# A transformer layer on one Trainium2 core: the conditioning's partial rows summed by transposes and a reduction, in a new SBUF layout

## The chip, the cores and the metric

The kernel runs on one core of one Trainium2 chip. Its engines work side by side, each on its own queue of instructions: TensorE (PE, matrix products into PSUM), VectorE (DVE), ScalarE (ACT), GpSimd (POOL, unused here) and SyncE (SP), which issues nearly all DMAs. The metric is the device time of one execution in microseconds, as the median of several runs. The profile is of one further execution, so its durations add up to its own time and not to the median.

## The reference, cut to what matters

One layer of an encoder in float32, 256 rows of width 2048: gated feed-forward (width 5632), a mixer with two groups of eight attention heads, and a second feed-forward. Each of the three is preceded by a normalisation with a shift and a scale and followed by a gate, and these nine vectors come from the conditioning vector `c`:

```python
cond = jax.nn.silu(c)                      # (1, 2048)
mod = cond @ w_ada[l] + b_ada[l]           # (1, 9 * 2048)
sh1, sc1, gt1, sh2, sc2, gt2, sh3, sc3, gt3 = jnp.split(mod, N_MOD, axis=-1)
h = modulate(rmsnorm(x, g_ffn1_pre[l]), sh1, sc1)
y = rmsnorm(swiglu(h, w1_gate[l], w1_up[l], w1_down[l]), g_ffn1_post[l])
x = x + MACARON_WEIGHT * gt1[:, None, :] * y
# the mixer with sh2, sc2, gt2 and the second feed-forward with sh3, sc3, gt3 follow
```

## The kernel before, in words

**Products.** The 256 rows are two tiles of 128. Weights arrive in units of 256 x 512 elements (512 KB, two rows of 2 KB in each partition) in `raw`, a ring of 8 slots. Each float32 product is made of three products of rounded operands: ACT copies a unit to a rounded high piece `w_hi` (a ring of 4, line 457), DVE subtracts it and leaves the low piece `w_lo` in the place of `raw` (line 771), and PE runs high x high, high x low and low x high (lines 1254 to 1256), 12 matmuls of 512 columns for a unit. The transposed activations stand in `h_hi`/`h_lo` or, within a feed-forward, in `hid_hi`/`hid_lo`. PE's results collect in the PSUM pairs `pair0` and `pair1`. PE waits for a unit on `raw_used`, which `lo_unit` raises on DVE.

**Stages.** A first stage ("pre", four parts) makes the first shift and scale; then gate/up 1 (11 blocks, the middle ones in a hardware loop), down 1 (4 blocks), input projection ("win", 8 blocks), the two small projections and attention, output projection ("wo", 4 blocks), gate/up 2 and down 2. At the end of down 1, of wo and of down 2 `branch_end` finishes the normalisation and the residual.

**The conditioning.** The product of `cond` with `w_ada` (151 MB of weights) is made on DVE, between the rest. Its 18432 columns are 36 quarters of 512, each with 8 units (kind "A" in the plan). For a unit `ada_unit` multiplies each of its two rows by a scalar of `c_col` and adds it to a 128 x 512 accumulator (lines 787 and 790). After 8 units the 128 partitions hold 128 partial rows, which must be added up over the partitions. For the 28 quarters behind the first stage the accumulator is `acc` (two slots), for the 8 of the first stage it is `start_acc` with two partial rows in each partition.

`sum_columns` on PE (line 1314) adds them up: it waits until DVE has taken the last unit, and for the previous sums to be used (`mod_ready`), and multiplies each 128 x 128 piece by a column of ones (line 1326). The result is one column of `mps` for a piece, so the vector comes out along the partitions, where it is needed. `mod_columns` on DVE (line 809) then adds the bias from `col` and writes to `mod` (line 820), and raises `mod_ready`. In the plan PE's part stands at the end of a block and DVE's part in the next one, before the low piece of unit 3 or 4.

**Order of the queues.** It is written out by hand. `run` on DVE walks through a block's units in the order of the DMAs, and calls tasks ahead of the unit they are listed for. `transposes` (line 1288) is the helper for all other transpositions on PE: the piece of data is loaded as weights and the identity `ident` streams through, into the two halves of `tps`.

**SBUF.** Tiles are placed one behind the other in the order of their declaration. 1152 bytes of each partition are taken before the first one, so `raw` starts at byte 1152. From the sizes, `w_hi` starts at 33920, `x` at 50304, `y` at 66688, `acc` at 87168, `h_hi` at 101664 and `hid_hi` at 134432. `start_acc` and the mixer's tiles share the place of `hid_hi` and `hid_lo`.

Of the kernel before, what the change touches and what calls it, by code (L numbers as in the profile page):

```python
# [23 lines left out]
BF16 = mybir.dt.bfloat16  # L24
ALU = mybir.AluOpType
ACT = mybir.ActivationFunctionType
AX_X = mybir.AxisListType.X

P = 128
SEQ = 256  # L30
TT = SEQ // P
D = 2048
KD = D // P
FF = 5632
Q_RANK, KV_RANK = 512, 256
NOPE, ROPE, DV = 128, 64, 128
HEADS = 8
CHUNK = 64
EPS = 1e-6
N_MOD = 9  # L40
# [3 lines left out]
DB = D // NB  # L44
# [6 lines left out]
C_ID, C_TRI, C_ONE = 0, P, 2 * P  # L51
C_COS, C_SIN = 3 * P, 3 * P + TT * ROPE // 2
C_ALL = 3 * P + TT * ROPE
# [4 lines left out]
V_ROWS = 246  # L58
# [120 lines left out]
def build(nc, A, const, out):  # L179
    pl, tp, taken, order = make_plan()  # L180
    ctx = ExitStack()
    with ctx:
        def sb(name, shape, dt=F32):
            return ctx.enter_context(nc.sbuf_tensor(name, shape, dt))
# [3 lines left out]

        with nc.sbuf_tensor("raw", [P, RING, 2, NB], F32) as raw:
            pass
        w_lo = sb("w_lo", [P, RING, 2, NB], F32R)
# [4 lines left out]
        s = sb("s", [P, TT, NB])  # L198
        acc = sb("acc", [P, 2, NB])
        tmp = sb("tmp", [P, 2, NB])  # L200
        cst = sb("cst", [P, C_ALL])
        msk = sb("msk", [P, 3, P], BF16)
        col = sb("col", [P, V_ROWS])
        mod = sb("mod", [P, N_MOD * KD])
        a_col = sb("a_col", [P, KD])
        g_col = sb("g_col", [P, KD])
        c_col = sb("c_col", [P, 2, KD])
        ssq = sb("ssq", [P, TT, DB])
        ms = sb("ms", [P, TT])
        inv_ms = sb("inv_ms", [P, TT])  # L210
        newton = sb("newton", [P, TT])
        warm = sb("warm", [P, 1])
        rstd = sb("rstd", [P, TT])
        kpe = sb("kpe", [P, 2, TT, ROPE])
        fz = sb("fz", [P, 5, TT, HEADS])
        nmax = sb("nmax", [P, 2, TT])
        nbias = sb("nbias", [P, 2, TT])
        rsum = sb("rsum", [P, 2, TT])
        rinv = sb("rinv", [P, 2, TT])
        ident = cst[:, C_ID:C_ID + P]  # L220
        tri = cst[:, C_TRI:C_TRI + P]
        ones = cst[:, C_ONE:C_ONE + P]

        h_hi = sb("h_hi", [P, KD, SEQ], F32R)
        h_lo = sb("h_lo", [P, KD, SEQ], F32R)
# [19 lines left out]
            pass  # L245
        hid_hi = sb("hid_hi", [P, FF // P, SEQ], F32R)
        hid_lo = sb("hid_lo", [P, FF // P, SEQ], F32R)
        gate_mix = kv[:, 0, :]


# [9 lines left out]
        mps = ctx.enter_context(nc.psum_tensor("mps", [P, 2, NB], F32))  # L260
# [55 lines left out]
        def plus(n, i, per):  # L316

            return n + i * per if per else n
# [447 lines left out]
        def _(dve):  # L766
# [42 lines left out]
            def mod_columns(b, i=0, per_q=0):  # L809

                k, c0 = DB * len(b.sums), plus(DB * b.sums[0], i, DB * per_q)
                dve.wait_ge(sum_ready, plus(b.m + 1, i, int(per_q > 0)))
                if b in pl["pre"]:

                    c0 = DB * pl["pre"].index(b)
                    of = lambda v: v[:, 0:2 * KD].rearrange("p (v k) -> p v k", v=2)[:, :, c0:c0 + DB]
                    nc.vector.tensor_tensor(of(mod), mps[:, 0, 0:k].rearrange("p (v k) -> p v k", v=2), of(col),
                                            ALU.add).then_inc(mod_ready, 1)
                    return
                nc.vector.tensor_tensor(mod[:, bass.ds(c0, k)], mps[:, 0, 0:k], col[:, bass.ds(c0, k)],  # L820
                                        ALU.add).then_inc(mod_ready, 1)

            def power(k, width, columns, t=slice(0, TT)):
# [159 lines left out]
            def quarter_columns(e):  # L983

                mod_columns(pre[e - 1])
                dve.drain()
                k = slice(DB * (e - 1), DB * e)
                nc.vector.scalar_tensor_tensor(a_col[:, k], mod[:, KD:2 * KD][:, k], 1.0,
                                               col[:, G_PRE["ffn1"]:G_PRE["ffn1"] + KD][:, k],
                                               ALU.add, ALU.mult).then_inc(gain_ready, 1)  # L990
                dve.drain()
                return mod[:, 0:KD]
# [20 lines left out]
            for f, gu, down in (("1", "gu1", "down1"), ("2", "gu2", "down2")):  # L1013
# [12 lines left out]
                for start, count in RUNS[gu]:  # L1026
                    before, b, at = pl[gu][start - 1], pl[gu][start], 2 * (start - 1)
                    with dve.Fori(0, count) as i:
                        def last_block():
                            hidden(before, i, 16, 1)  # L1030
                            if before.sums and (b.sums or count == 1):
                                mod_columns(before, i, 1)

                        def last_hidden():
                            lo_hid(tp["hid" + f] + at, th + at, (i + (start - 1)) * 4, i, 2)
                        run(b, {4: last_block, 7: last_hidden}, i, len(b.seq), 16)
# [9 lines left out]
                if f == "1":  # L1046
                    mod_columns(last)
# [134 lines left out]
                for t in range(TT):  # L1182
                    q = y[:, t, 0:HEADS * QK].rearrange("p (h e) -> p h e", h=HEADS)
                    q1, q2 = q[:, :, NOPE:NOPE + half], q[:, :, NOPE + half:QK]
                    c, d = (v[:, t:t + 1, :].to_broadcast([P, HEADS, half]) for v in (cos, sin))
# [7 lines left out]
                for n in range(N_ATT + 6):  # L1193
# [13 lines left out]
                    if 0 <= m < N_ATT:  # L1207
# [3 lines left out]
                        for t in range(TT):  # L1211
                            k0, k1 = (0, P) if t == 0 else (P, 3 * P)
                            ins = nc.vector.tensor_scalar(prob[:, m % 4, k0:k1], prob[:, m % 4, k0:k1],
                                                          rinv[:, m % 2, t:t + 1], None, ALU.mult)
# [30 lines left out]
        def _(pe):  # L1245
# [68 lines left out]
            def sum_columns(b, i=0, per=0, per_m=0, start=None):  # L1314

                pe.wait_ge(raw_used, plus(b.r_sums(), i, per))
                if per_m or b.m:
                    pe.wait_ge(mod_ready, plus(b.m, i, per_m))
                for k in range(DB * len(b.sums)):
                    c = slice((k % 4) * P, (k % 4 + 1) * P)  # L1320
                    if start is None:
                        parts = [acc[:, b.slots[k // 4], c]]
                    else:
                        parts = [start[:, k // 4, row, c] for row in range(2)]
                    for n, part in enumerate(parts):
                        ins = nc.tensor.matmul(mps[:, 0, k:k + 1], part, ones[:, 0:1], start=n == 0,  # L1326
                                               stop=n == len(parts) - 1)
                ins.then_inc(sum_ready, 1)

            def gate_rows(t0, dg0, places):  # L1330
# [23 lines left out]
            nc.tensor.transpose(mps[:, 1, P:V_ROWS], y[0:rest, 0, P:2 * P], cst[0:rest, 0:rest]).then_inc(cols_full, 1)  # L1354
            pre = pl["pre"]
            sum_columns(pre[0], start=start_acc[:, 0])

            for e, b in enumerate(pre[1:] + pl["gu1"][:1]):
                for cp in (2 * e, 2 * e + 1):
                    turn_x(tp["mod1"], XN["ffn1"], cp)  # L1360
                for u in range(4):
                    cp = 2 * e + u % 2
                    pe.wait_ge(h_ready, HR["ffn1"] + cp + 1)
                    unit(b, u, h_hi, h_lo, 2 * cp, u // 2, cp == 0, cp == 7)
                if b.sums:
                    sum_columns(b, start=start_acc[:, (e + 1) % 2])

            for f, gu, down in (("1", "gu1", "down1"), ("2", "gu2", "down2")):
                first, t0 = pl[gu][0], tp["hid" + f]
                if f == "2":  # L1370
                    gate_up(first, ready=HR["ffn2"], ahead=lambda u: turn_ahead(tp["mod2"], XN["ffn2"], u))
                    sum_columns(first)
                pe.wait_ge(t_taken["a"], taken[t0 - 1][1])
                for start, count in RUNS[gu]:
                    before, b, at = pl[gu][start - 1], pl[gu][start], 2 * (start - 1)
# [31 lines left out]
                for n, b in enumerate(win):  # L1407
                    bank_free(b.g)
                    for u in range(8):
                        if n == 0:  # L1410
# [3 lines left out]
                             n=KV_RANK + ROPE + HEADS if n == 1 else NB)  # L1414
                        if n and u == (7 if n <= 3 else 5):
# [16 lines left out]
                            if n == 5:  # L1432
# [6 lines left out]
                                                 stop=True).then_inc(cum_full, 1)  # L1439
# [166 lines left out]
```

## Time and profile before

| | before |
|---|---|
| median of 3 runs | 2041.19 us (2041.05 to 2043.98) |
| profiled execution | 2044.09 us |
| its span | 2042.3 us |
| PE, DVE, ACT busy | 95%, 67%, 41% |
| mean granted PE clock | 0.981 |
| DMA | 488.20 MB, 239 GB/s over the span |

The span is the time between the first and the last instruction of the profile; 1.8 us of the profiled execution lie around it. Matmuls are pipelined, so that the durations of several overlap: one 128x512 matmul is recorded with some 0.39 us while the next one starts 0.23 us after it. What PE's queue pays is read from start to start, or from the chain of waits, where each piece ends with the start of the next. A group in the chain with "x8" has eight records. A time in brackets in the timeline is the engine's idle time before the instruction, and behind the arrow stands what ended it.

### The profile page before, as it was taken

The page shows a single profiled execution, that of the slowest core. Times are in us where ns is not written, and L with a number is a line of the kernel's source. Part 1 is how long each engine was busy: PE and PEld are TensorE (multiplying, and loading weights), DVE is VectorE, ACT ScalarE, POOL GpSimd, SP SyncE. Part 2 cuts the span into 40 slices and gives each one's busy share as a digit, 9 for nine tenths or more (in the row PEclk, how much of TensorE's full clock was granted, in tenths as well). Part 3 has the DMA queues.
Part 4 walks back from the last instruction along what each step waited for, and adds up shares of the span by engine and source line. Part 5 has one row for each costly group of instructions (what it writes and reads, how often), then busy time and mean ns, then how long its engine had stood idle before and what let it go on. Part 6 is the DMA issues. An engine that isn't in the chain of part 4 may idle for free.

```text
span 2042.3 us, 24582 instructions
## 1 busy us (share of the span) xinstructions
PE 1935.3 (95%) x8662; PEld 1560.7 (76%) x8662; DVE 1359.0 (67%) x1707; ACT 846.7 (41%) x1040; POOL 0.2 (0%) x4
## 2 busy tenths in 40 slices
PE   1779999999999999989999997999999999999998
PEld 1568888888887888767887776788888888788886
DVE  6877777777777667778885886777644444544444
ACT  3134433444343334354434545534344444344433
POOL 0000000000000000000000000000000000000000
PEclk9879999999999999989999998999999999999999
DMA  9878878888888778849885385787766666656663
GB/s 363 315 272 264 264 260 272 273 276 270 278 270 277 264 259 307 299 125 310 287 301 183 107 277 185 248 267 258 266 183 183 183 183 184 184 174 186 186 188 131
DMA packets 254921, 488.20 MB, mean 239 GB/s; under 512 B 17414, under 2 KB 19836, under 8 KB 254588
## 3 DMA queue, kind: packets, MB, share of 16 engines
q1 hardware_dynamic: 253968, 486.66, 72.9%
q8 instruction: 46, 0.75, 0.1%
q10 hardware_dynamic: 876, 0.53, 0.1%
q14 instruction: 31, 0.25, 0.0%
HBM read 485.04 MB, written 2.10 MB: 239 GB/s over the span
## 4 chain that ended last, share of the span: by engine, by line
PE 87%; DVE 6%; DMA 3%; DVEq 2%; ACT 1%; issue 1%; ACTq 0%; SPq 0%
PE pair L1256 28%; PE pair L1254 28%; PE pair L1255 27%; PE tps L1294 2%; DMA raw<-in_w_ada 2%; DVE start_acc L790 1%; DVEq L779 1%; PE mps L1326 1%; DVE w_lo L771 1%; DVE acc L790 1%; DMA raw<-in_w_in 1%; ACT w_hi L457 1%; PE tps L1334 0%; DMA raw<-in_w_up 0%; DVEq L1202 0%
## 5 line engine op out<-in xcount | busy, mean ns | idle before, releaser
L771 DVE TENSOR_TENSOR w_lo<-raw,w_hi 128x1024 fp32r<-128x1024 f32 x634 | 770.5, 1219 | 528.6 <-ACT w_hi L457 525.0
L457 ACT ACTIVATE w_hi<-raw 128x1024 fp32r<-128x1024 f32 x634 | 668.1, 1056 | 1021.2 <-PE pair L1256 551.8
L1254 PE MATMUL pair<-w_hi,h_hi 128*128 128x512 f32 (+1 forms) x1792 | 715.6, 399 | 38.7 <-DVE w_lo L771 36.6
L1256 PE MATMUL pair<-w_hi,h_lo 128*128 128x512 f32 (+1 forms) x1792 | 714.5, 399 | 0.0
L1255 PE MATMUL pair<-w_lo,h_hi 128*128 128x512 f32 (+1 forms) x1792 | 708.4, 395 | 0.0
L1254 PEld LDWEIGHTS pair<-w_hi,h_hi 128*128 128x128 f32 x1792 | 340.3, 190 | 121.8 <-issue 39.7
L1255 PEld LDWEIGHTS pair<-w_lo,h_hi 128*128 128x128 f32 x1792 | 340.3, 190 | 82.0 <-issue 0.2
L1256 PEld LDWEIGHTS pair<-w_hi,h_lo 128*128 128x128 f32 x1792 | 339.7, 190 | 79.7
L790 DVE SCALAR_TENSOR_TENSOR acc<-raw,c_col,acc 128x512 f32<-128x512 f32 x420 | 315.7, 752 | 53.1 <-DMA raw<-in_w_ada 20.6
L1256 PE MATMUL pair<-w_hi,hid_lo 128*128 128x512 f32 x704 | 279.6, 397 | 0.0
L1254 PE MATMUL pair<-w_hi,hid_hi 128*128 128x512 f32 x704 | 278.4, 395 | 0.6 <-DVE w_lo L771 0.6
L1255 PE MATMUL pair<-w_lo,hid_hi 128*128 128x512 f32 x704 | 277.2, 394 | 0.0
L1254 PEld LDWEIGHTS pair<-w_hi,hid_hi 128*128 128x128 f32 x704 | 132.2, 188 | 34.5 <-DVE w_lo L771 3.9
L1255 PEld LDWEIGHTS pair<-w_lo,hid_hi 128*128 128x128 f32 x704 | 132.2, 188 | 32.4
L1256 PEld LDWEIGHTS pair<-w_hi,hid_lo 128*128 128x128 f32 x704 | 132.1, 188 | 31.6
L790 DVE SCALAR_TENSOR_TENSOR start_acc<-raw,c_col,start_acc 128x512 f32<-128x512 f32 x112 | 79.2, 749 | 12.5 <-DMA raw<-in_w_ada 7.9
L1294 PE MATMUL tps<-cst,y 128*128 128x128 f32 (+1 forms) x188 | 34.3, 321 | 23.8 <-DVE y L854 18.0
L1294 PEld LDWEIGHTS tps<-cst,y 128*128 128x128 f32 (+1 forms) x188 | 26.8, 166 | 31.2 <-issue 10.5
L1326 PE MATMUL mps<-cst,start_acc 128*128 128x1 f32 x128 | 19.7, 288 | 22.8 <-DVE start_acc L790 22.8
L1326 PEld LDWEIGHTS mps<-cst,start_acc 128*128 128x128 f32 x128 | 19.4, 243 | 24.1 <-DVE start_acc L790 24.1
L938 DVE TENSOR_TENSOR hid_lo<-tps,hid_hi 128x512 f32 (+1 forms) x44 | 28.4, 683 | 7.9 <-ACT hid_hi L535 7.6
L932 DVE TENSOR_TENSOR s<-s,pair 128x512 f32<-128x512 f32 x44 | 28.1, 681 | 3.7 <-PE pair L1256 3.7
(156 smaller groups left out, 660.5 us busy)
## 6 DMA issues: line engine op xcount, KB each, us to landing
raw<-in_w_ada SPq DMA_DIRECT2D x288, 512.0 KB, 4.7
raw<-in_w_gate SPq DMA_DIRECT2D x176, 512.0 KB, 3.9
raw<-in_w_up SPq DMA_DIRECT2D x176, 512.0 KB, 3.9
raw<-in_w_down SPq DMA_DIRECT2D x176, 512.0 KB, 3.8
raw<-in_w_in SPq DMA_DIRECT2D x56, 512.0 KB, 4.5
raw<-in_w_o SPq DMA_DIRECT2D x32, 512.0 KB, 5.0
raw<-in_w_uq SPq DMA_DIRECT2D x6, 512.0 KB, 4.7
raw<-in_w_in SPq DMA_DIRECT2D x8, 320.0 KB, 3.0
```

What stands on the lines that cost most here:

```text
L457: nc.scalar.activation(w_hi[:, w % HI_RING, :, 0:n], raw[:, r % RING, :, 0:n], ACT.Copy).then_inc(hi_ready, 1)
L771: nc.vector.tensor_tensor(w_lo[:, r % RING, :, 0:n], raw[:, r % RING, :, 0:n], w_hi[:, w % HI_RING, :, 0:n], ALU.subtract).then_inc(raw_us ...
L779: dve.drain()
L790: ins = nc.vector.scalar_tensor_tensor(total, raw[:, r % RING, k, :], c_col[:, 1, j:j + 1], total, ALU.mult, ALU.add)
L932: ins = nc.vector.tensor_tensor(s[:, t, :], s[:, t, :], pair[g % 2][:, t, :], ALU.mult)
L938: nc.vector.tensor_tensor(hid_lo[:, bass.ds(c0 + 2 * k, 2), :], tps[:, (t0 + k) % 2, :].rearrange("p (c t) -> p c t", c=2), hid_hi[:, bass ...
L1254: nc.tensor.matmul(o, hi, wh, start=first and kk == 0, stop=False)
L1255: nc.tensor.matmul(o, hi, wl, start=False, stop=False)
L1256: ins = nc.tensor.matmul(o, lo, wh, start=False, stop=last and kk == 1)
L1294: ins = nc.tensor.transpose(tps[0:rows, n % 2, k * P:(k + 1) * P], src, ident)
L1326: ins = nc.tensor.matmul(mps[:, 0, k:k + 1], part, ones[:, 0:1], start=n == 0, stop=n == len(parts) - 1)
```

## The change

In `sum_columns`, where the accumulator is `acc`, each 128 x 128 piece is now transposed into its own 128 columns of `mps`, in place of the product with a column of ones. A quarter fills one half of `mps` (one PSUM bank). In `mod_columns` DVE sums each piece along its columns with a `tensor_reduce` to four columns of the new small tile `ada_sum`, drains, and adds the bias from there. The first stage (`start_acc`) is left as it was.

The tiles `mod`, `a_col`, `g_col`, `ada_sum`, `c_col` and `ssq` (896 bytes together) are declared ahead of `raw`, so that this starts at byte 2048, and `cst`, `msk`, `col` and the other small ones behind all the large ones. With this every large tile starts on a multiple of 2048 bytes.

```diff
@@ -188,6 +188,13 @@
+        mod = sb("mod", [P, N_MOD * KD])
+        a_col = sb("a_col", [P, KD])
+        g_col = sb("g_col", [P, KD])
+        ada_sum = sb("ada_sum", [P, 2 * DB])
+        c_col = sb("c_col", [P, 2, KD])
+        ssq = sb("ssq", [P, TT, DB])
+
         with nc.sbuf_tensor("raw", [P, RING, 2, NB], F32) as raw:
             pass
         w_lo = sb("w_lo", [P, RING, 2, NB], F32R)
@@ -198,28 +205,6 @@
         tmp = sb("tmp", [P, 2, NB])
-        cst = sb("cst", [P, C_ALL])
-        msk = sb("msk", [P, 3, P], BF16)
-        col = sb("col", [P, V_ROWS])
-        mod = sb("mod", [P, N_MOD * KD])
...
@@ -245,6 +230,24 @@
         hid_lo = sb("hid_lo", [P, FF // P, SEQ], F32R)
+
+        cst = sb("cst", [P, C_ALL])
+        msk = sb("msk", [P, 3, P], BF16)
+        col = sb("col", [P, V_ROWS])
...
@@ -817,7 +820,11 @@
-                nc.vector.tensor_tensor(mod[:, bass.ds(c0, k)], mps[:, 0, 0:k], col[:, bass.ds(c0, k)],
+                for j in range(len(b.sums)):
+                    nc.vector.tensor_reduce(ada_sum[:, j * DB:(j + 1) * DB],
+                                            mps[:, j, :].rearrange("p (c k) -> p c k", c=DB), AX_X, ALU.add)
+                dve.drain()
+                nc.vector.tensor_tensor(mod[:, bass.ds(c0, k)], ada_sum[:, 0:k], col[:, bass.ds(c0, k)],
                                         ALU.add).then_inc(mod_ready, 1)
@@ -1319,12 +1326,12 @@
                     if start is None:
-                        parts = [acc[:, b.slots[k // 4], c]]
-                    else:
-                        parts = [start[:, k // 4, row, c] for row in range(2)]
-                    for n, part in enumerate(parts):
-                        ins = nc.tensor.matmul(mps[:, 0, k:k + 1], part, ones[:, 0:1], start=n == 0,
-                                               stop=n == len(parts) - 1)
+
+                        ins = nc.tensor.transpose(mps[:, k // 4, c], acc[:, b.slots[k // 4], c], ident)
+                        continue
+                    for row in range(2):
+                        ins = nc.tensor.matmul(mps[:, 0, k:k + 1], start[:, k // 4, row, c], ones[:, 0:1],
+                                               start=row == 0, stop=row == 1)
                 ins.then_inc(sum_ready, 1)
```

## Rows read from the trace of the kernel before

**Rows 1.** The page: PE's busy time, and the chain by engine.

```profile
PE 1935.3 (95%) x8662; PEld 1560.7 (76%) x8662; DVE 1359.0 (67%) x1707; ACT 846.7 (41%) x1040; POOL 0.2 (0%) x4
...
PE 87%; DVE 6%; DMA 3%; DVEq 2%; ACT 1%; issue 1%; ACTq 0%; SPq 0%
```

**Rows 2.** Windows: busy us by engine (instructions), PE clock, DMA share, GB/s.

```profile
136.00:860.00 724.00, 722.34 (x3177) 581.15 (x3178) 521.27 (x586) 293.93 (x314) 0.00 (x0) 1.00 0.81 271
...
960.00:1110.00 150.00, 148.84 (x685) 120.45 (x684) 110.68 (x141) 68.87 (x83) 0.00 (x0) 1.00 0.84 276
```

**Rows 3.** Waits in 0 to 136 us: total, times, longest.

```profile
PE pair L1254 <- DVE w_lo L771: 31.1, 6, 8.9
```

**Rows 4.** Groups and sources: large matmuls (page, busy, mean ns, idle), and the sums.

```profile
L1254 PE MATMUL pair<-w_hi,h_hi 128*128 128x512 f32 (+1 forms) x1792 | 715.6, 399 | 38.7 <-DVE w_lo L771 36.6
...
L1254 PE MATMUL pair<-w_hi,hid_hi 128*128 128x512 f32 x704 | 278.4, 395 | 0.6 <-DVE w_lo L771 0.6
...
L1326 PE MATMUL mps<-cst,acc x224: 165/250/250, 196.6 to 1462.5; 128*128 128x1 f32 x112
```

**Rows 5.** Chain that ended last: start us, length us; first and last sum.

```profile
196.77 0.79 PE mps L1326 x8
197.55 0.34 PE pair L1254
...
1462.01 0.79 PE mps L1326 x8
```

**Rows 6.** Chain and source: four transposes between matmuls, four behind others, durations.

```profile
894.68 0.44 PE tps L1294 x4
895.11 0.23 PE pair L1254
...
1107.98 0.67 PE tps L1294 x4
...
L1294 PE MATMUL tps<-cst,s x208: 270/273/329, 159.3 to 1787.3; 128*128 128x128 f32 x104
```

**Rows 7.** DVE: reductions from PSUM by form; timeline behind an addition in gate/up.

```profile
L1201 DVE TENSOR_REDUCE nmax<-pair 128x1 f32<-128x256 f32 x16 | 6.6, 414 | 0.0
...
L1201 DVE TENSOR_REDUCE nmax<-pair 128x1 f32<-128x128 f32 x16 | 4.5, 284 | 1.9 <-PE pair L1485 1.9
...
201.59 1.23 DVE L771 TENSOR_TENSOR w_lo<-raw,w_hi 128x1024 fp32r<-128x1024 f32 x1 [1.20 <-ACT w_hi L457]
```

**Rows 8.** Timeline at the branch end behind down 1, DVE and PE.

```profile
879.51 0.16 DVE L820 TENSOR_TENSOR mod<-mps,col 128x8 f32<-128x8 f32 x1
...
880.55 0.16 DVE L831 TENSOR_REDUCE ms<-ssq 128x2 f32<-128x4 f32 x1 [0.89 <-ACT tmp L468]
880.79 0.17 DVE L833 TENSOR_SCALAR ms<-ms 128x2 f32<-128x2 f32 x1
...
883.12 0.45 PE L1294 MATMUL tps<-cst,y 128*128 128x128 f32 x1 [8.35 <-DVE y L854]
```

**Rows 9.** Timeline in the output projection's second block, PE and DVE.

```profile
1189.33 0.47 PE L1254 MATMUL pair<-w_hi,h_hi 128*128 128x512 f32 x1 [0.21 <-DVE w_lo L771]
...
1199.92 1.22 DVE L771 TENSOR_TENSOR w_lo<-raw,w_hi 128x1024 fp32r<-128x1024 f32 x1
...
1203.41 0.39 PE L1254 MATMUL pair<-w_hi,h_hi 128*128 128x512 f32 x1
```

**Rows 10.** Operands at other addresses: durations (shortest, median, longest), and groups.

```profile
L1505 PE MATMUL mps<-y,fv x16: 275/275/275, 1127.2 to 1145.7; 128*128 128x128 f32 x16
...
L790 DVE SCALAR_TENSOR_TENSOR acc<-raw,c_col,acc 128x512 f32<-128x512 f32 x420 | 315.7, 752 | 53.1 <-DMA raw<-in_w_ada 20.6
...
L790 DVE SCALAR_TENSOR_TENSOR start_acc<-raw,c_col,start_acc 128x512 f32<-128x512 f32 x112 | 79.2, 749 | 12.5 <-DMA raw<-in_w_ada 7.9
```

**Rows 11.** Windows in the first stage, `x` arriving and `raw` alone; columns as rows 2.

```profile
15.00:24.00 9.00, 0.00 (x0) 0.00 (x0) 4.38 (x8) 4.48 (x8) 0.00 (x0) 1.00 1.03 397
...
35.00:50.00 15.00, 8.80 (x40) 8.40 (x40) 13.11 (x29) 9.98 (x17) 0.00 (x0) 1.00 1.05 387
```

More of the change, by code:

```diff
@@ L200, in build @@
         tmp = sb("tmp", [P, 2, NB])
-        cst = sb("cst", [P, C_ALL])
-        msk = sb("msk", [P, 3, P], BF16)
-        col = sb("col", [P, V_ROWS])
-        mod = sb("mod", [P, N_MOD * KD])
[L205 to L222, printed above, removed]
         h_hi = sb("h_hi", [P, KD, SEQ], F32R)
@@ L247, in build @@
         hid_lo = sb("hid_lo", [P, FF // P, SEQ], F32R)
+        cst = sb("cst", [P, C_ALL])
+        msk = sb("msk", [P, 3, P], BF16)
+        col = sb("col", [P, V_ROWS])
+        ms = sb("ms", [P, TT])
+        inv_ms = sb("inv_ms", [P, TT])
+        newton = sb("newton", [P, TT])
+        warm = sb("warm", [P, 1])
+        rstd = sb("rstd", [P, TT])
+        kpe = sb("kpe", [P, 2, TT, ROPE])
+        fz = sb("fz", [P, 5, TT, HEADS])
+        nmax = sb("nmax", [P, 2, TT])
+        nbias = sb("nbias", [P, 2, TT])
+        rsum = sb("rsum", [P, 2, TT])
+        rinv = sb("rinv", [P, 2, TT])
+        ident = cst[:, C_ID:C_ID + P]
+        tri = cst[:, C_TRI:C_TRI + P]
+        ones = cst[:, C_ONE:C_ONE + P]
         gate_mix = kv[:, 0, :]
```

## Prediction

> **What bounds the kernel now.** I read the page first. TensorE (PE) is busy 95% of the span, and the chain that ended last is PE for 87%, DVE (VectorE) 6%, DMA 3% [rows 1]. The windows by stage say where this holds: from 136 to 860 us PE is busy 722 of 724 us with the clock at 1.00, and from 960 to 1110 us 149 of 150 [rows 2]; the weak places are the first stage, the branch ends and the attention stage. So nearly every nanosecond that the PE queue gets shorter in the long stages is a nanosecond of the end time, while DVE work counts only where it makes PE wait. The waits agree: PE's first product waited 36.6 us for low weight pieces in all [rows 4], 31.1 of it before 136 us [rows 3]; after that DVE is ahead. The reader should keep two prices in mind: what a step costs PE's queue (start to start, since matmuls overlap), and how much idle time lies on DVE before the next thing that PE needs.
>
> **Part 1, TensorE: 112 one-column matmuls become 112 transposes.** `sum_columns` without `start` handles 28 quarters (512 columns of the conditioning each): 36 quarters in all, 8 of them in the first stage, which keep their matmuls. A quarter has four pieces of 128x128. Today each piece is a matmul against a column of ones, and it shows as two records (224 for 112), a quarter as "x8" [rows 4]. On the chain a quarter takes 0.79 us, and the first large matmul behind it 0.34 us where the others take 0.23 [rows 5]: the step costs 0.79 + 0.34 - 0.23 = 0.90 us of PE's queue. A transpose of a 128x128 f32 piece from SBUF is already in the kernel, one record each: four of them between large matmuls take 0.44 us on the chain, and the next matmul takes 0.23 [rows 6]. So a quarter would cost 0.44 us, and the gain is 0.90 - 0.44 = 0.46 us.
>
> How many of the 28 are on the path: the chain holds "mps L1326 x8" or "x16" for ten quarters in gate/up 1, four in down 1 (one of the three entries is x16), five in the input projection, two in the output projection and four in gate/up 2; first and last are in [rows 5]. That is 25. The three left are the last pair of down 1, where PE idles afterwards for 8.35 us anyway [rows 8], and the one of the attention stage, behind which PE waits for a low piece (0.21 us) [rows 9]. Part 1: 25 x 0.46 = -11.5 us. The bound on the poor side is the dearest group of four transposes on the chain, 0.67 us with a full fill before it [rows 6]: gain 0.23 each, -5.8 us. I take 0.44, because that row stands between full-width matmuls as the new ones will. Below 0.44 there is no row.
>
> A rule of the Trainium skill speaks against this part: "TensorE: Matmul & The Clock Gate", Part 4: PE-mode transpose, gives about 275 ns for one transpose inside a kernel. The trace agrees with that as a duration (median 273 ns [rows 6]), but the durations overlap, and it is the spacing, 0.44 / 4 = 0.11 us, that the queue pays.
>
> **Part 2, VectorE: 28 reductions more, and a drain.** `mod_columns` gets one `tensor_reduce` from PSUM, 128x512 to four columns, for each quarter. The trace has no such width; the max reductions from PSUM take 284 ns for 128 columns and 414 ns for 256 [rows 7], 130 ns per 128 columns, so 414 + 260 = 674 ns (an estimate from these two rows). The drain adds about 0.08 us, the gap between two small dependent operations [rows 8]. All of it is 28 x 0.674 + 26 x 0.08 = 21.0 us of DVE time. What is queued behind it is the next `lo_unit`, and for that waits PE.
> - Gate/up: `mod_columns` runs behind the product of the hidden block, and DVE idles 1.20 us right after it until ScalarE delivers the high piece [rows 7]. 0.75 us fit in. Cost nothing. If that cover were gone, the low piece would still be needed only after four units of PE (each 12 matmuls of 0.233 us, 2.8 us).
> - Down 1 has the same pattern, and after the last gate/up block DVE next waits for ScalarE's high hidden pieces.
> - Output projection, the tightest: DVE is almost never idle in its second block. The low piece ready at 1199.92 + 1.22 = 1201.14 us is used by PE at 1203.41 [rows 9]; the reserve is 2.27 us against a delay of 0.75. Nothing. The input projection is similar with a larger reserve.
> - Branch end after down 1: two quarters. The addition starts at 879.51 us, DVE then idles 0.89 us for ScalarE's squares and goes on at 880.55 with the mean square, and PE is waiting [rows 8]. With two reductions and the drain it would be over at 879.51 + 1.35 + 0.08 + 0.16 = 881.10: +0.6 us on the path.
> PE's next `sum_columns` waits for `mod_ready`, but that comes a whole block later (46 us in gate/up). Part 2: +0.6 us; the bounds are 0.6 and 21.0.
>
> **Part 3, the layout.** The first large tile starts at byte 1152 of a partition, and `raw`, `w_hi`, `x`, `y`, `s`, `acc` and `tmp` all lie at 1152 modulo 2048, `h_hi`, `hid_hi` and the mixer tiles at 1312. Moving 896 bytes of small tiles ahead brings all of them to 0. No instruction is added. Does an engine care? The middle matmul of an attention output (line 1505) streams a 512-byte slice of `y` that crosses a 2 KB line for every other head (byte 1664) and doesn't for the others (1152), and shortest, median and longest are all 275 ns [rows 10]. On DVE, `acc` (same offset as `raw`) takes 752 ns and `start_acc` (160 bytes off) 749 [rows 10]. So for engines I take 0. For a bound either way there is no row with full-width matmuls at another address; each nanosecond on one would be 3 x (1792 + 704) = 7488 ns, 7.5 us [rows 4].
> For DMA, `raw` goes from 128 to 0 modulo 256. DMA holds 3% of the chain, 61 us [rows 1], two thirds of it in the first stage. Rows of 2 KB arrive at 387 GB/s with the queues full; while `x` with its 8 KB rows comes in between, at 397 [rows 11]. A cheaper write of 2 KB rows is therefore bounded by 2.6% of 61 us, 1.6 us, from rows. All destinations lie at 128 modulo 256, so nothing here shows an effect of alignment, and I take 0.
>
> **Sum.** -11.5 + 0.6 + 0 = -10.9 us. The profiled execution took 2044.09 us (span 2042.3 and 1.8 around it), so 2033.2; the median of the runs is 2.9 us lower, 2041.19, and the same difference gives 2030.3 us.
>
> **Rivals.**
> 1. *DMA writes get cheaper with the 256-byte alignment.* For it: the queues are full at the start (share 1.05). Against: much of these 61 us is latency and the order of the queue. By rows -1.6 us more: 2028.7. The Trainium skill, "DMA: Bandwidth & Descriptors", How a descriptor splits into AXI transactions, says that a descriptor off a 256-byte boundary needs one transaction more, 68 beats for 64 here; an estimate from that page is 5.9% of the DMA pieces, -3.6 us, 2026.7. No row here shows it.
> 2. *The transposes don't overlap*, each paying its duration: 4 x 0.273 = 1.09 us against 0.90, +0.19 x 25 = +4.8 us, with the branch end +5.4: 2046.6. The entry of 0.44 us for four speaks against it. Milder: 0.67 us a quarter, 2041.2 - 5.8 + 0.6 = 2036.0.
> 3. *The reductions come to light on DVE (the slower side).* In the stages with conditioning loads DVE is busy 72% (136 to 860 us) and 74% (960 to 1110 us) [rows 2], in places much more, and the low pieces are the last thing that PE needs. If all 21.0 us showed, 2041.2 - 11.5 + 21.0 = 2050.7. It ends slower from the point where more than 11.5 us, 16 of the 28, are uncovered. Against it: the idle gaps and the reserve of 2.27 us just shown.
> 4. *The gain meets the transfers.* ScalarE waits for weights to land, not for PE, in much of down 1, input and output projection. If these 11 quarters gave nothing, 2030.3 + 5.1 = 2035.4. Against it: loads are issued when PE frees a slot, so they move with PE, and they run at 271 to 276 GB/s there [rows 2], below 387 [rows 11].
> 5. *The layout changes the pace of every matmul.* One nanosecond faster gives 2022.8, one slower 2037.8, two slower 2045.3. The Trainium skill, "TensorE: Matmul & The Clock Gate", Wait — 56ns, not 53.3ns?, gives 215.7 ns start to start for 512 columns; the trace has 233, so there is something that could go, up to 131 us by that page, but no row ties it to addresses.
>
> **Chances.** Forecast 0.51; rival 1 0.18; rival 4 and the mild form of 2 together 0.12; rival 5 faster 0.05, slower by about a nanosecond 0.04 (ends within 0.2%) and by more 0.03; rival 3 0.05 (half of it within 0.2%), full form of 2 0.02. A measurement of this kernel can tell about 0.2%, 4.1 us, from no change. Faster (under 2037.1) 0.86, same 0.065, slower 0.075. The range reaches from rival 1 in full with two microseconds to spare, 2024.5, to rival 5 at one nanosecond, 2038.
>
> **What would show it.** In the profile after: 112 transposes from `acc` into `mps` at 0.44 us a quarter on the chain, the matmul behind at 0.23; a gate/up block shorter by 0.46 us (46.6 now, PE's 192 large matmuls and the small ones); 28 reductions of about 0.67 us, with PE's wait for low pieces after 136 us unchanged at 5.5 us; large matmuls still 0.233 us apart; the first stage within 1.5 us of its present end. I would be wrong if the spacing of the large matmuls moved, if a quarter stayed at 0.8 us, or if PE waited for DVE in the projections.

## The result, and the profile after

| | before | after |
|---|---|---|
| median of the runs on the same chip | 2042.59 us (2041.05 to 2044.19) | 1988.86 us (1984.76 to 1993.20) |
| ratio after / before | | 0.9737, 95% interval 0.9713 to 0.9761 |
| profiled execution (span) | 2044.09 us (2042.3) | 1990.05 us (1988.3) |
| mean granted PE clock | 0.981 | 0.981 |

The kernel became 2.6% faster, and the profiled execution 54.0 us shorter, five times the 10.9 us of the forecast. The direction was right, and the time lies far below the range. The clock is the same in both. First the page of after: PE's busy time and the chain, to be read against [rows 1], and the large matmul whose row stood in [rows 4] (in after it is line 1261; the two others of a step are 1262 and 1263).

```profile
PE 1878.7 (94%) x8550; PEld 1546.7 (78%) x8550; DVE 1377.0 (69%) x1735; ACT 847.4 (43%) x1040; POOL 0.2 (0%) x4
...
PE 85%; DVE 7%; DMA 3%; DVEq 3%; ACT 1%; issue 1%; ACTq 0%; SPq 0%
...
L1261 PE MATMUL pair<-w_hi,h_hi 128*128 128x512 f32 (+1 forms) x1792 | 707.8, 395 | 37.6 <-DVE w_lo L774 35.4
```

PE is busy 56.6 us less, of which the 112 records that are gone can explain only a part, while the mean durations of the large matmuls fell by 3 to 8 ns (the one shown from 399 to 395). The durations overlap, so the place to look is the chain. Here is the end of two blocks of gate/up 2 that hold no conditioning and no wait: start and length of the eight transpositions that close a block, of before and then of after.

```profile
1562.66 0.87 PE tps L1294 x8
1608.33 0.87 PE tps L1294 x8
```

```profile
1566.14 0.87 PE tps L1301 x8
1610.58 0.88 PE tps L1301 x8
```

A block is 45.67 us before and 44.44 after. Between the two ends lie 192 large matmuls and nothing else, so their spacing went from (45.67 - 0.87) / 192 = 233.3 ns to (44.44 - 0.87) / 192 = 226.9 ns. No instruction of this block was edited; what changed for it is where its tiles lie.

The sums behaved as foretold. Chain, sources and timeline of after (start us, length us; durations shortest, median and longest in ns), which answer to [rows 5], [rows 6] and [rows 8]:

```profile
195.23 0.44 PE mps L1330 x4
195.67 0.24 PE pair L1261
...
L1330 PE MATMUL mps<-cst,acc x112: 270/272/273, 195.1 to 1424.4; 128*128 128x128 f32 x112
...
L824 DVE TENSOR_REDUCE ada_sum<-mps x28: 681/684/692, 198.7 to 1428.1; 128x4 f32<-128x512 f32 x28
...
857.22 0.19 ACT L471 ACTIVATION_READ_ACCUMULATOR tmp<-x 128x1 f32 x1
...
857.83 0.15 DVE L838 TENSOR_REDUCE ms<-ssq 128x2 f32<-128x4 f32 x1
```

Four transposes take 0.44 us of the queue. At the branch end behind down 1 the mean square starts 0.42 us after ScalarE's last square has ended (857.41); before, it started 0.02 us after it (880.55 and 880.53).

### The profile page after: what moved, and what is told of

Its sections match the earlier page's. It is cut to its first block, busy times and chain, and to the rows that moved or that the text cites. A ratio compares the mean times of both kernels' runs of the same rounds, so it can differ in the third digit from the quotient of the medians.

```text
span 1988.3 us, 24412 instructions
## 1 busy us (share of the span) xinstructions
PE 1878.7 (94%) x8550; PEld 1546.7 (78%) x8550; DVE 1377.0 (69%) x1735; ACT 847.4 (43%) x1040; POOL 0.2 (0%) x4
## 4 chain that ended last, share of the span: by engine, by line
PE 85%; DVE 7%; DMA 3%; DVEq 3%; ACT 1%; issue 1%; ACTq 0%; SPq 0%
PE pair L1261 27%; PE pair L1263 27%; PE pair L1262 27%; PE tps L1301 2%; DVEq L782 2%; DVE start_acc L793 2%; DMA raw<-in_w_ada 2%; DVE w_lo L774 2%; DVE acc L793 1%; DMA raw<-in_w_down 1%; PE mps L1330 1%; PE tps L1341 1%; ACT w_hi L460 0%; DVE x L970 0%; DMA raw<-in_w_in 0%
## 5 line engine op out<-in xcount | busy, mean ns | idle before, releaser
L1261 PE MATMUL pair<-w_hi,h_hi 128*128 128x512 f32 (+1 forms) x1792 | 707.8, 395 | 37.6 <-DVE w_lo L774 35.4
L1263 PE MATMUL pair<-w_hi,h_lo 128*128 128x512 f32 (+1 forms) x1792 | 700.3, 391 | 0.0
L1262 PE MATMUL pair<-w_lo,h_hi 128*128 128x512 f32 (+1 forms) x1792 | 700.2, 391 | 0.0
L1263 PE MATMUL pair<-w_hi,hid_lo 128*128 128x512 f32 x704 | 274.1, 389 | 0.0
L1301 PE MATMUL tps<-cst,y 128*128 128x128 f32 (+1 forms) x188 | 34.3, 321 | 24.8 <-DVE y L861 19.1
L519 ACT ACTIVATE tmp<-tps,mod,a_col 128x256 f32<-128x256 f32 x30 | 15.2, 557 | 36.4 <-DVE a_col L995 26.8
```

The costliest lines, as they stand in the source:

```text
L1261: nc.tensor.matmul(o, hi, wh, start=first and kk == 0, stop=False)
L1262: nc.tensor.matmul(o, hi, wl, start=False, stop=False)
L1263: ins = nc.tensor.matmul(o, lo, wh, start=False, stop=last and kk == 1)
L1301: ins = nc.tensor.transpose(tps[0:rows, n % 2, k * P:(k + 1) * P], src, ident)
```

## The experiments

Each kernel ran beside the kernel before on the same chip. The ratio is to that. A kernel with no interval was run once, with its profile. "Cycles" are the mean distance from start to start of large matmuls that follow each other without a gap, times 2.4: the granted clock is 1.00 in these stretches, which is the level of 2.4 GHz. They are given for the stages that use `h_hi`/`h_lo` and for those that use `hid_hi`/`hid_lo`. "Distance" is where the activation tile (`h_hi` or `hid_hi`, loaded as weights) starts, less where `w_hi` (which streams) starts, modulo 256 bytes. `raw`/`w_lo` and `w_hi` share one offset throughout, `h_hi` and `h_lo` too, and `hid_hi` and `hid_lo`, except where a text says otherwise.

| kernel | distance h / hid | cycles h / hid | time us | ratio (95%) |
|---|---|---|---|---|
| before | 160 / 160 | 560.1 / 560.1 | 2042.59 | 1 |
| after | 0 / 0 | 544.4 / 544.5 | 1988.86 | 0.9737 (0.9713 to 0.9761) |
| layout_only | 0 / 0 | 544.7 / 544.5 | 1999.83 | 0.9778 (0.9761 to 0.9796) |
| sums_only | 192 / 192 | 549.3 / 549.3 | 2003.10 | 0.9801 (0.9783 to 0.9818) |
| stationary_off | 160 / 160 | 560.1 / 560.1 | 2030.64 | 0.9936 (0.9915 to 0.9956) |
| moving_off | 128 / 128 | 557.9 / 557.8 | 2026.58 | 0.9910 (0.9894 to 0.9927) |
| pad_32 | 192 / 192 | 549.4 / 549.5 | 2013.41 | 0.9857 (0.9841 to 0.9874) |
| sums_still | 160 / 160 | 560.1 / 560.3 | 2031.69 | 0.9949 (0.9933 to 0.9966) |
| all_128 | 0 / 0 | 544.6 / 544.2 | 1990.91 | 0.9742 (0.9726 to 0.9759) |
| map_192_384 | 192 / 128 | 549.6 / 557.9 | 2009.06 | one run |
| map_64_256 | 64 / 0 | 559.6 / 544.6 | 2017.66 | one run |
| map_128_320 | 128 / 64 | 558.4 / 560.1 | 2027.49 | one run |
| map_32_1024 | 32 / 0 | 559.6 / 544.4 | 2019.23 | one run |
| raw_160 | only `raw`/`w_lo` off | 555.9 / 555.8 | 2018.14 | one run |
| whi_160 | only `w_hi` off | 557.4 / 557.4 | 2021.22 | one run |
| hlo_160 | only `h_lo`, `hid_lo` off | 559.6 / 560.0 | 2031.69 | one run |
| down_spread | 0 / 0 | 544.8 / 544.1 | 1987.60 | 0.9731 (0.9718 to 0.9745) |
| after_again | 0 / 0 | 544.4 / 544.8 | 1989.93 | 0.9739 (0.9725 to 0.9752) |

### The two parts alone

layout_only is after with the old sums:

```diff
-                        ins = nc.tensor.transpose(mps[:, k // 4, c], acc[:, b.slots[k // 4], c], ident)
+                        parts = [acc[:, b.slots[k // 4], c]]
...
-                    nc.vector.tensor_reduce(ada_sum[:, j * DB:(j + 1) * DB],
...
```

> The new layout with the old sums (one-column matmuls, no reduction). If the layout sets the spacing of the large matmuls, they are 226.7 ns apart here as in the changed kernel, 7488 x 6.7 ns = 50 us are gained less what the transfers give back: 1995 to 2003 us, and a gate/up block takes 45.3 us. If the spacing came with the transposes (the rival), this kernel stays at 233.3 ns and 2036 to 2042 us.

Measured: 44.9 us less than before (2044.68 on its chip), 544.7 cycles, both as expected for the case that the layout sets the spacing. The layout alone brings most of the gain.

sums_only is before with the new sums, and `ada_sum` declared ahead of `c_col`:

```diff
+        ada_sum = sb("ada_sum", [P, 2 * DB])
         c_col = sb("c_col", [P, 2, KD])
```

> The old layout with the new sums. This is the part that the prediction costed: spacing 233.3 ns, 0.46 us less a quarter, 2030.3 us by its sum. If the spacing came with the transposes, 226.7 ns and under 1995 us. If the reductions on VectorE cost more than priced, above 2036 us.

Measured: 41.6 us less. By itself this would say that the sums bring nearly as much as the layout, and the two gains would add up to 86 us, where both together brought 54. The trace shows why it is no clean test: the spacing had moved too, to 549.3 cycles, in blocks without any sum. `c_col` stands between the large tiles in the old layout, so the 32 bytes of `ada_sum` had shifted `h_hi`, `h_lo` and all behind them. The miss pointed at the cause: addresses matter in steps far below 2 KB.

### Which tile, and against what

stationary_off and moving_off are after with unused bytes: 160 ahead of `h_hi`, or 1152 ahead of `raw` and 896 behind `w_hi`.

```diff
+        pad_h = sb("pad_h", [P, 40])
         h_hi = sb("h_hi", [P, KD, SEQ], F32R)
```

> The changed kernel with 160 bytes put ahead of h_hi, so that the operands that PE loads as weights (h_hi, h_lo, hid_hi, hid_lo, the mixer's tiles) lie 160 bytes off the 2 KB grid and the streamed ones (w_hi, w_lo) on it. If the stationary operand's place, or the distance between the two operands modulo 2 KB, costs the time: 233.3 ns and about 2035 us. If only the streamed operand counts: 226.7 ns and 1989 us.

> The changed kernel with raw/w_lo and w_hi alone at 1152 modulo 2048 as before (1152 bytes ahead of raw, 896 behind w_hi), all others on the grid. If the streamed operand's place costs the time: spacing 233.3 ns and 2028 to 2033 us. If the stationary one does: 226.7 ns and 1989 us. The DMA's destinations are again at 128 modulo 256: if that alone slows the transfers, the windows of the first stage fall from 408 to some 387 GB/s.

Measured: 560.1 and 557.9 cycles (233.4 and 232.5 ns), and times some 4 and 1 us shorter than the nearest that were expected. Either shift alone takes most of the gain back. The ends of two blocks of stationary_off on the chain, 45.68 us apart:

```profile
1548.40 0.87 PE tps L1302 x8
1594.08 0.87 PE tps L1302 x8
```

With `h_hi` back at 160 the spacing is that of before to a tenth of a cycle, although `raw` and `w_hi` stay on the 2 KB grid. In moving_off the activations stay on the grid. So neither place alone decides.

The next three separate the distance from the grid. pad_32 is before with 32 unused bytes and no other change. sums_still is before with the new sums and `ada_sum` behind the last large tile, so that nothing moves. all_128 is after with 128 bytes ahead of everything, so that no large tile is on the grid but their distances stay 0.

```diff
+        pad_a = sb("pad_a", [P, 2 * DB])
         c_col = sb("c_col", [P, 2, KD])
```

> The kernel before with one unused tile of 32 bytes ahead of c_col and nothing else: c_col and what stands behind it up to hid_lo move by 32 bytes (h_hi from 1312 to 1344 modulo 2048), raw and w_hi stay at 1152. Theory: what counts is the distance, modulo some power of two, between the tile that PE streams and the tile that it loads as weights at the same time (160 bytes before, 192 here, as in sums_only): spacing 549 cycles of 2.4 GHz (228.9 ns) in place of 560, and 2041 - 7488 x 4.5 ns = some 2008 us. Rival: the spacing in sums_only came with the transposes; then this kernel stays at 2041 us.

> The new sums in the old layout with ada_sum behind hid_lo, so that no other tile moves: the part of the change that the prediction costed, without the 32 bytes that sums_only had moved. By the sum of the prediction 2030 us, spacing 233.3 ns. If the transposes themselves speed up the large matmuls, some 2003 us as sums_only.

> The changed kernel with 128 bytes ahead of raw: every large tile lies 128 bytes off the 2 KB grid, and at the same distance from each other as in the changed kernel. If the distance counts: spacing 226.7 ns and 1989 us, and a little more, as DMA writes to 128 modulo 256 again (387 in place of 408 GB/s at the start). If each 2 KB row that crosses a 2 KB line costs: some 233 ns and 2027 us as moving_off.

Measured: 32 unused bytes make the kernel 1.4% faster (2013.41 against 2043.01) and give the same 549.4 cycles as sums_only. sums_still gives back a ratio of 0.9949, 11.3 us, with the spacing as before. all_128 is as fast as after (0.9742 and 0.9737). pad_32 had the spacing that was expected of it, but 2008 us were expected and it took 2013.41: some 4 us of the 33 that the spacing gives didn't reach the end. The ends of blocks on the chain, of pad_32, sums_still and all_128:

```profile
1540.00 0.87 PE tps L1295 x8
1584.82 0.87 PE tps L1295 x8
```

```profile
1549.73 0.87 PE tps L1299 x8
1595.40 0.87 PE tps L1299 x8
```

```profile
1566.65 0.87 PE tps L1302 x8
1611.07 0.87 PE tps L1302 x8
```

Blocks of 44.82, 45.67 and 44.42 us: 228.9, 233.3 and 226.8 ns a matmul. So the 2 KB boundary makes no difference to the spacing (226.8 ns off it, 226.9 on it); that PE's tiles share an offset does. For the sums, the chain of sums_still in gate/up 1, where a block holds one quarter:

```profile
193.83 0.44 PE mps L1328 x4
...
239.94 0.44 PE mps L1328 x4
```

46.11 us from sum to sum, where before has 46.57 (two blocks from 196.77 to 289.90 us): the 0.46 us of the forecast.

### How far the distance counts

The four map kernels are after with `h_hi`/`h_lo` and `hid_hi`/`hid_lo` moved by the two numbers of their names. One of them:

```diff
+        pad_h = sb("pad_h", [P, 48])
         h_hi = sb("h_hi", [P, KD, SEQ], F32R)
...
+        pad_m = sb("pad_m", [P, 48])
```

> The changed kernel with h_hi and h_lo 192 bytes off the grid and hid_hi and hid_lo 384 bytes off, raw and w_hi on it. If the distance alone counts, the stages on h have the pattern of sums_only (distance 192: 549 cycles mean, one of three matmuls free) and the down stages that of moving_off (distance 896, 384 modulo 512: 558 cycles). If the absolute places count, some other pattern.

> The changed kernel with h_hi, h_lo 64 bytes and hid_hi, hid_lo 256 bytes off the grid of raw and w_hi. So far distances of 0, 160, 192, 384 and 896 bytes gave a mean spacing of 544, 560, 549, 558 and 558 cycles, the same for all slices of 512 bytes. If the period of the effect is 256 bytes, the down stages are at 544 here; if it is 128, the distance 64 costs as 192 did (549) ; if it is 512, both cost something, 548 to 560.

> The changed kernel with h_hi, h_lo 128 bytes and hid_hi, hid_lo 320 bytes off. Period 256: 128 costs as 384 (558) and 320 as 64 does. Period 128: 128 is free (544), which 384 being dear already speaks against. Period 512: two new values.

> The changed kernel with h_hi, h_lo 32 bytes and hid_hi, hid_lo 1024 bytes off. The slices of a tile lie 512 bytes apart and all cost the same, so a distance of 1024 should be free (544 cycles); if the 2 KB grid itself counts, it is dear (some 558). For 32 bytes: if half a 64-byte line is what makes 160 dearer than 192 (560 against 549), it costs some 10 cycles; if only whole steps of 64 bytes count, none.

Measured, in cycles: 32 gives 560, 64 gives 560, 128 gives 558, 192 gives 549.6, 256 and 1024 give 544.5 as 0 does, 320 gives 560 as 64, 384 gives 558 as 128. So the cost depends on the distance modulo 256 bytes, among the values tried. It isn't in proportion to it, and the two directions differ: 192 is cheaper than 64. The guesses about steps of 64 bytes fell: 32 bytes cost as much as 64 and 160, where nothing or 10 cycles had been expected.

That 512 bytes is a period also follows from one kernel: the 128-column slices of `h_hi` start 512 bytes apart, and in before the spacings of the same matmul of a step agree within 2 cycles from slice to slice. That 256 is one rests on the map.

### Which of the four tiles

A step has three matmuls: `w_hi` streams against `h_hi`, `w_lo` against `h_hi`, `w_hi` against `h_lo`. The weights of the next are loaded while one streams: in after, the first product of a step (line 1261) has its load start at 1570.07 us, together with the third product of the step before (line 1263), and take 0.19 of the 0.23 us until it starts itself. One theory was that the cost falls on the step whose streamed tile and whose next weights are out of line. raw_160, whi_160 and hlo_160 are after with one of the tiles alone moved by 160 bytes (`h_lo` and `hid_lo` together). Of whi_160:

```diff
+        pad_w = sb("pad_w", [P, 40])
         w_hi = sb("w_hi", [P, HI_RING, 2, NB], F32R)
...
+        pad_x = sb("pad_x", [P, 472])
         x = sb("x", [P, TT, D])
```

> The changed kernel with raw (and w_lo in its place) alone 160 bytes off the grid, w_hi and the weights' side on it. Of the three matmuls of a product one streams w_lo. If the cost lies in the overlap of a stream with the weight load that runs beside it, only the step behind the w_lo matmul gets longer, the mean to 548 to 550 cycles, and the time is some 2005 us; if the distance between the DMA's and PE's tiles counts in another way, all three or none.

> The changed kernel with w_hi alone 160 bytes off (raw, w_lo and the weights' side on the grid). With w_lo alone off all three steps got longer, 556 cycles in the mean, although the two others stream w_hi beside loads at distance 0. If each stream is compared with the loads beside it alone, two of three steps cost here, 13 and 23 as before, and the third none. If a step already costs because a neighbouring stream lies elsewhere, all three cost again, 555 to 560.

> The changed kernel with h_lo and hid_lo alone 160 bytes off. One of three weight loads comes from them. If only the load that runs beside a stream counts, one step of three costs 12 to 23 cycles and the mean is 548 to 552. If any tile out of line makes all steps cost, 555 to 560.

Measured, cycles from one start to the next behind the first, the second and the third matmul of a step (stages with `h_hi`):

| | behind hi x hi | behind lo x hi | behind hi x lo |
|---|---|---|---|
| after | 544 | 544 | 544 |
| before | 557 | 556 | 567 |
| distance 192 (sums_only) | 555 | 544 | 550 |
| raw_160 | 557 | 555 | 555 |
| whi_160 | 548 to 556 | 554 to 566 | 556 to 564 |
| hlo_160 | 562 | 561 | 556 |

In whi_160 the steps on a unit's first and on its second row differ, and both values are given. One tile out of line, and all three get longer, also those whose own operands are in line with each other. With the theory of the load beside the stream at least one of the three should have stayed at 544, and a mean of 548 to 552 was expected of raw_160 and hlo_160 by it, where 556 and 560 came. It fell. What is shown is the rule in bytes. What in PE or in its path to SBUF makes it, no run here shows, and it stays open.

### Where part of the gain stays behind

Spacing and sums should give 7488 x 6.54 + 10.9 = 59.9 us (6.54 ns is 15.7 cycles), and the profiled executions differ by 54.0. The stages, from the first to the last start of a large matmul, before and after, with what (matmuls x 6.54 ns + quarters x 0.46 us) gives:

| | before | after | shorter by | expected |
|---|---|---|---|---|
| gate/up 1 (its first product starts in the first stage) | 563.3 | 547.1 | 16.2 | 18.4 |
| down 1 | 251.3 | 245.4 | 5.9 | 8.7 |
| input projection | 190.3 | 184.3 | 6.0 | 7.3 |
| wo and gate/up 2 | 623.1 | 606.5 | 16.6 | 19.1 |
| down 2, no conditioning | 246.3 | 239.3 | 7.0 | 6.9 |

Where no conditioning is loaded the whole gain arrives. The other four stages miss 8.8 us together, and the stretches between the stages are some 2 us shorter than before. Down 1 misses most for its length, and there the chain of after goes through transfers twice, where before had one such piece, of 6.56 us at 835.85 (a second profile of after, after_again, has one as well, of 6.96 us at 759.12):

```profile
629.19 6.57 DMA raw<-in_w_down
...
690.73 6.75 DMA raw<-in_w_down
```

down_spread is after with the 12 conditioning units of a down 1 block no longer in a row:

```diff
-    pl["down1"] = [Block(at, pattern(22, list(range(4, 16))), 1, at["a"] // 8 - (n % 2)) for n in range(DB)]
+    pl["down1"] = [Block(at, pattern(22, [4, 5, 7, 8, 10, 11, 13, 14, 16, 17, 19, 20]), 1, at["a"] // 8 - (n % 2)) for n in range(DB)]
```

> The changed kernel with the twelve conditioning units of a down 1 block spread over units 4 to 20 in place of 4 to 15. With a unit of weights and one of conditioning for each 2.72 us of PE the transfers are asked for 385 GB/s there, and two waits of 6.6 and 6.8 us for in_w_down stand on the chain. If these hold back the gain, down 1 gets 2 to 3 us shorter (245.4 us from its first to its last large matmul now, 242.4 expected) and the time is 1986. If the waits only replace others, down 1 keeps its 245 us.

> The changed kernel as it is, beside down_spread on the same chip: 1989 us, 0.974 of the kernel before; spacing 544 cycles, down 1 245 us.

Measured: down 1 took 242.1 us (242.4 expected) against 243.8 in after_again, and the input projection 187.4 against 185.6. But two profiles of the same kernel, after and after_again, differ by nearly as much: 245.4 and 243.8 us, 184.3 and 185.6. The total, 0.9731 against 0.9739, can't be told apart. One transfer still stands on the chain (831.07, 4.69 us). So another order in down 1 brought nothing that shows at the end. It may be that it passes a shortage on to the next stage, and that the bytes which this stretch must load set the limit; neither is shown, and a kernel with fewer bytes wasn't run.

## Why the prediction was right or wrong, point by point

**What bounds the kernel: right, and worth more than was drawn from it.** PE's queue sets the end, so the 6.54 ns that a matmul got shorter are worth 7488 x 6.54 = 49.0 us, of which layout_only, with the old sums, brought 44.9 to the end.

**Part 1: right.** 0.44 us a quarter for the transposes and 0.24 for the matmul behind them (0.44 and 0.23 were taken). sums_still measured both parts together at 11.3 us between medians (7 to 14 by its interval), against 10.9. The duration of a transpose is 272 ns and its place in the queue 110 ns, so pricing by durations, rival 2, would have made a loss of this gain. Its milder form, 0.67 us a quarter, didn't come either.

**Part 2: right.** A reduction takes 684 ns (674 estimated), the delay at the branch end is 0.4 us (0.6), and after 136 us PE waits 36.7 - 29.5 = 7.2 us for low pieces, where before had 37.2 - 31.1 = 6.1 (the prediction's 5.5 leaves out the 0.6 us of the `hid_hi` products in [rows 4]). Rival 3 stays away: these waits are only 1.1 us longer, although PE's products now follow each other faster. Before over the span (its part up to 136 us is in [rows 3]), then after over the span and from 0 to 136 us:

```profile
PE pair L1254 <- DVE w_lo L771: 37.2, 17, 8.9
```

```profile
PE pair L1261 <- DVE w_lo L774: 36.7, 17, 8.2
...
PE pair L1261 <- DVE w_lo L774: 29.5, 6, 8.2
```

**Part 3: the step that failed** is "So for engines I take 0", argued from [rows 10]. The term that it put at nothing measured 6.54 ns a matmul, 49.0 us in the sum. The argument was weak in three ways:
- The attention matmul stood there with its duration, though the prediction itself says that what PE's queue pays is read from start to start. Durations gauge that poorly: those of the large matmuls fell by 3 to 8 ns, depending on the matmul, and the spacing by 6.5.
- Its two kinds of operand lay 512 bytes apart. 1664 and 1152 are the same modulo 256 (both 128), so the row never varied what counts. It answered whether a 2 KB line matters, and for PE it doesn't; it left open whether the distance between two tiles does.
- The row for DVE says nothing of how PE reads.

The figures for the right question stood in the same paragraph: `w_hi` at 1152 and `h_hi` at 1312 modulo 2048, 160 bytes apart before, and 0 after.

**Rival 5 was the mechanism, at the wrong size.** It was given one or two nanoseconds, up or down, 7.5 us for each, and a chance of 0.05 for faster. The rate was right, and the size was 6.5 ns. The low bound of the range came from DMA alone, and at 2024.5 us it left out even the 2022.8 us that rival 5 gives for one nanosecond; an unknown with 7488 uses and no row on it ought to have widened the range. No kernel that was run had a spacing below 226.7 ns (544 cycles). The Trainium skill, "TensorE: Matmul & The Clock Gate", Wait — 56ns, not 53.3ns?, has 215.7 ns from start to start for 512 columns. The traces here don't reach that figure: of the 17.6 ns over it in before, 6.5 belong to the tiles' distance, and 11 stay unexplained in every kernel run.

**Rival 1: the effect is there, and bought nothing that shows.** A window of the first stage, with the columns of [rows 11], of after and then of all_128, whose destinations are at 128 modulo 256 like those of before:

```profile
24.00:35.00 11.00, 0.25 (x2) 0.25 (x2) 10.33 (x18) 1.29 (x2) 0.00 (x0) 1.00 1.05 408
```

```profile
24.00:35.00 11.00, 0.00 (x0) 0.00 (x0) 10.08 (x16) 1.29 (x2) 0.00 (x0) 1.00 1.05 387
```

With the queues full, rows of 2 KB arrive at 408 GB/s in place of 387, 5.4% more. All the kernels agree in this window: those with `raw` at 0 modulo 256 have 407 or 408 GB/s, and those with it at 128 (before, sums_only, moving_off, pad_32, sums_still, all_128) or at 160 (raw_160) have 387. The next window, 35 to 50 us, gives part of it back: 375 in after against 386 in all_128, at a share of 1.01 in place of 1.05, so the queues were no longer full all the time. all_128 and after end within each other's intervals, so at the end of the kernel it is worth nothing measurable. The Trainium skill, "DMA: Bandwidth & Descriptors", How a descriptor splits into AXI transactions, gives a rule for where a read may start, from which the prediction worked out an estimate of 5.9% less time for a transfer. The traces come near it for an SBUF destination: 387 to 408 GB/s is 5.1% less time.

**Rival 4: true in part.** Some 6 us of the 59.9 didn't reach the end, and the stages that miss it are those with conditioning to load. The rival was priced for the 11 quarters alone (5.1 us), while here the gain of the faster matmuls is cut too. That transfers are the cause is argued from the chain of down 1, and no run shows it.

## What to carry to other kernels

Print where every tile that TensorE reads starts, modulo 256 bytes, and give streamed and loaded tiles the same remainder (these runs show it for float32 operands rounded as here and 512 columns; other types and widths weren't tried). A single small tile declared between large ones can break it, and a block without waits, divided by its matmuls, shows whether it is right. When a change moves addresses, treat the pace of the most frequent instruction as an unknown with that count in front of it, and look for a row in which the address really differs in the way in question. And when one part of a change is tested alone, compare the spacing in a block that this part doesn't touch, before believing the difference in time.

## What the runs showed of the hardware

- The spacing of matmuls of 128x128 by 512 columns, on rounded float32 operands with new weights for each, depends on the addresses of their operands relative to each other: 544 cycles at distance 0 modulo 256 bytes, 549 at 192, 558 at 128, 560 at 32, 64 and 160. Why is open.
- One tile of four out of line (`w_lo`, `w_hi`, or the low activations) costs nearly as much, 556 to 560, and in all three matmuls of a step.
- 32 unused bytes, which brought the distance from 160 to 192, made this kernel 1.4% faster. An offset shared by all tiles costs nothing: 128 bytes off the grid gave 544.6 and 544.2 cycles.
- A destination at 0 modulo 256 bytes took DMA rows of 2 KB at 408 GB/s with the queues full, one at 128 or 160 at 387. The kernel's time didn't show it.
- Four transposes of 128x128 between large matmuls take 0.44 us of PE's queue, 0.11 us each, where one is recorded with 272 ns.
- A VectorE sum from PSUM of 128x512 float32 to 128x4 took 684 ns.
